# A hybrid layer and a conformer block on one core: another opening, with the norms as two numbers a row

## The reference, cut to what matters

```
h = rms_norm(x, pre_g)                       # x / sqrt(mean(x^2) + 1e-6) * g
a_u, a_v, a_g, b_x, b_g, x_q, x_g, gates = split(h @ w_in)
y_a = u * spatial_gating(layer_norm(a_v)) * silu(a_g)
y_b = s5(b_x) ... * silu(b_g)                # diagonal state space model, GLU
k, v = rms_norm(mem, mem_g) @ w_k, ... @ w_v # 4 heads of 256
y_x = softmax(x_q k^T / 16) v * silu(x_g)
x = x + rms_norm(sum(sigmoid(gates) * (y @ w_branch)) @ w_out, post_g)
then: x += conformer_conv(rms_norm(x)); x += sq_relu_mlp(rms_norm(x)); out = rms_norm(x)
```

## Time and profile before

| | |
|---|---|
| median of 3 runs | 2095.28 us (2091.62 to 2097.49) |
| the profiled execution | 2091.96 us, span 2090.2 us |
| PE busy | 2013.0 us, 96% |
| DVE, ACT, POOL busy | 1610.0, 976.4, 417.4 us |
| chain that ended last | PE 68%, DVE 23%, issue 4%, ACT 3% |
| mean DMA rate | 181 GB/s |

### The profile page before, as it was taken

The page is one execution under the profiler, slowest core; times in us unless marked ns, Lnnn a source line. Parts: engine busy times, 40 slices in busy tenths (PEclk is TensorE's granted clock), DMA queues, the critical chain, the costliest instruction groups (busy, mean ns, idle before and its releaser), DMA issues.

```text
span 2090.2 us, 30805 instructions
## 1 busy us (share of the span) xinstructions
PE 2013.0 (96%) x12118; PEld 1750.6 (84%) x12118; DVE 1610.0 (77%) x2538; ACT 976.4 (47%) x1439; POOL 417.4 (20%) x293
## 2 busy tenths in 40 slices
PE   7999999999989999999999999999999999999997
PEld 6787887788777788888799987888888888888886
DVE  7766888989899996687899984777567657756766
ACT  5544444444443445556544335544344434434442
POOL 3400233333333330000187754000000000000000
PEclk9999999999999999999999998999999999999998
DMA  7554554444444455566456654555555555555553
GB/s 290 203 181 161 191 182 161 141 162 154 162 149 160 153 182 181 189 213 201 154 168 192 204 184 145 185 188 191 191 191 189 188 190 190 192 191 188 189 190 119
DMA packets 106704, 378.01 MB, mean 181 GB/s; under 512 B 11968, under 2 KB 15808, under 8 KB 106560
## 3 DMA queue, kind: packets, MB, share of 16 engines
q1 hardware_dynamic: 106560, 376.04, 53.9%
HBM read 373.01 MB, written 2.98 MB: 180 GB/s over the span
## 4 chain that ended last, share of the span: by engine, by line
PE 68%; DVE 23%; issue 4%; ACT 3%; DMA 1%; SPq 0%; DVEq 0%; ACTq 0%
PE bank L1751 37%; PE bank L1753 19%; DVE wl L991 7%; DVE bank L1536 3%; ACT wh L635 2%; PE bank L1740 1%; PE bank L1742 1%; PE bank L1741 1%; PE bank L1756 1%; PE bank L1758 1%; PE bank L1757 1%; DVE scr L1022 1%; PE bank L1780 1%; DVE wm L1315 1%; DVE sq L998 1%
## 5 line engine op out<-in xcount | busy, mean ns | idle before, releaser
L991 DVE TENSOR_TENSOR wl<-raw,wh 128x1024 fp32r<-128x1024 f32 x593 | 742.2, 1256 | 335.2 <-ACT wh L635 334.1
L635 ACT ACTIVATE wh<-raw 128x1024 fp32r<-128x1024 f32 x680 | 710.7, 1054 | 517.4 <-PE bank L1753 369.7
L1751 PE MATMUL bank<-Hr,wh 128*128 128x512 f32 x2432 | 864.8, 399 | 15.8 <-DVE wl L991 12.1
L1751 PE MATMUL bank<-Yr,wh 128*128 128x512 f32 x2176 | 768.5, 397 | 20.9 <-DVE wl L991 12.2
L1753 PE MATMUL bank<-Hr,wl 128*128 128x256 f32 x2432 | 683.9, 281 | 0.0
L1753 PE MATMUL bank<-Yr,wl 128*128 128x256 f32 x2176 | 610.6, 281 | 0.0
L1751 PEld LDWEIGHTS bank<-Hr,wh 128*128 128x128 f32 x2432 | 458.4, 188 | 133.5 <-issue 12.7
L1751 PEld LDWEIGHTS bank<-Yr,wh 128*128 128x128 f32 x2176 | 409.7, 188 | 119.8 <-DVE wl L991 11.3
L1753 PEld LDWEIGHTS bank<-Hr,wl 128*128 128x128 f32 x2432 | 462.1, 190 | 0.3
L1753 PEld LDWEIGHTS bank<-Yr,wl 128*128 128x128 f32 x2176 | 412.6, 190 | 0.2
L578 POOL TENSOR_TENSOR wl<-raw,wh 128x1024 fp32r<-128x1024 f32 x87 | 215.4, 2485 | 417.5 <-ACT wh L635 388.5
(11 more groups left out here) (321 smaller groups left out, 1815.6 us busy)
## 6 DMA issues: line engine op xcount, KB each, us to landing
raw<-in_w_up SPq DMA_DIRECT2D x128, 512.0 KB, 3.2
raw<-in_w_dn SPq DMA_DIRECT2D x128, 512.0 KB, 3.3
raw<-in_w_g SPq DMA_DIRECT2D x96, 512.0 KB, 3.2
raw<-in_w_p SPq DMA_DIRECT2D x80, 512.0 KB, 3.3
raw<-in_w_b SPq DMA_DIRECT2D x48, 512.0 KB, 3.3
raw<-in_w_out SPq DMA_DIRECT2D x32, 512.0 KB, 3.3
raw<-in_w_bx SPq DMA_DIRECT2D x16, 512.0 KB, 5.2
raw<-in_w_q SPq DMA_DIRECT2D x16, 512.0 KB, 3.4
```

Of the source, the lines that this page charges most:

```text
L635: e.activation(wh[:, c % WN, :], raw[:, c % RAW, :], ACT.Copy).then_inc(s_hi, 1)
L991: e.tensor_tensor(wl[:, c % RAW, :], raw[:, c % RAW, :], wh[:, c % WN, :].bitcast(F32), ALU.subtract).then_inc(s_low_v, 1)
L1751: e.matmul(dst.rearrange("p (h t) -> p h t", h=2), lh, pair.both[:, :, k, :], start=first_part and kk == 0, stop=last_part and kk == 7, sk ...
```

## The change

The DMAs at the start go x 0-3, chunk 0, x 4-7, chunks 1, 2, x 8-11, chunk 3, x 12-15, chunks 4 to 6, constants. ACT does x 0-3, high(0), x 4-7, high(1), high(2), x 8-11, high(3), high(4), x 12-15, and all four squares at c = 1 and 2. The squares are folded only from 16 to 4 tiles, the two folds being hung on c = 3 and 4 (mem: 21 and 22); PE sums the rest with eight matmuls of one column (`mean_squares`, in front of chunk 6; mem: 23), which leaves one number per token on the partitions, two columns. Epsilon, root and reciprocal work on these 128 x 2 numbers; DVE puts them on a diagonal (`across`), PE spreads them over the partitions by one product with `ones` (in front of chunk 7; mem: 24) and ACT copies this as r_x or r_mem. q reads `hp0` like bx, and the norm is multiplied onto its results. bx tiles 0 to 2 get their norm at c = 8. The scaling of x runs at c = 8 to 13, 15, 17, 19, 21, that of mem at c = 30 to 39.

```
-RX = 5
-MEM_SQ, MEM_R = 17, 23
-MEM_N = 26
+RX = 7
+X_N = (8, 9, 10, 11, 12, 13, 15, 17, 19, 21)
+MEM_SQ, MEM_R = 17, 24
+MEM_N = 30
 # SP
         e.dma_start(Xf[:, 0:4, :], a["xT"][:, 0:4, :]).then_inc(s_x[0], 16)
+        chunk(0)
         e.dma_start(Xf[:, 4:8, :], a["xT"][:, 4:8, :]).then_inc(s_x[1], 16)
-        chunk(0)
         chunk(1)
+        chunk(2)
         e.dma_start(Xf[:, 8:12, :], a["xT"][:, 8:12, :]).then_inc(s_x[2], 16)
-        chunk(2)
+        chunk(3)
         e.dma_start(Xf[:, 12:16, :], a["xT"][:, 12:16, :]).then_inc(s_x[3], 16)
...
 # ACT
+        def norm_across(n, dst):
+            w.wait_ge(s_rb, n)
+            e.activation(dst, bank[7][:, 0:T], ACT.Copy, scale=2048.0).then_inc(s_rstd, 1)
...
             elif j.stage == "q":
-                w.wait_ge(s_hl, 8)
+                w.wait_ge(s_hl, 4)
...
+            for c in ((0,), (1, 2), (3, 4), ())[i]:
+                high(c)
...
+            if c in (1, 2):
+                for i in (2 * c - 2, 2 * c - 1):
+                    e.activation(sq0[:, 4 * i:4 * i + 4, :], Xf[:, 4 * i:4 * i + 4, :], ACT.Square).then_inc(s_xq, 1)
...
+            if c == RX:
+                w.wait_ge(s_cst, 16)
+                norm_across(1, r_x)
+            if c == RX - 1:
+                root(1, rs_x)
...
-                w.wait_ge(s_mm, end("bx", 7))
+                w.wait_ge(s_mm, end("q", 7))
                 e.activation(mp.hi[:, u:u + 2, :], Mf[:, u:u + 2, :], ACT.Copy).then_inc(s_mh, 1)
 # DVE
+        def squares_folded(n):
+            w.wait_ge(s_xq, 4 * n)
+            e.tensor_tensor(sq0[:, 0:8, :], sq0[:, 0:8, :], sq0[:, 8:16, :], ALU.add).then_inc(s_v, w.own())
+            yield
+            w.wait_ge(s_v, w.n)
+            e.tensor_tensor(sq0[:, 0:4, :], sq0[:, 0:4, :], sq0[:, 4:8, :], ALU.add).then_inc(s_sum, 1)
+
+        def norm_rows(n, v):
+            w.wait_ge(s_mean, n)
+            e.tensor_scalar(v, bank[7][:, 0:2], 1e-6, None, ALU.add).then_inc(s_eps, 1)
+            w.wait_ge(s_root, n)
+            e.reciprocal(v, v).then_inc(s_v, w.own())
+            w.wait_ge(s_v, w.n)
+            w.wait_ge(s_id, 1)
+            across(v, 0, s_xdg)
+
+        def times_norm(j):
+            w.wait_ge(s_comb, j.comb)
+            w.wait_ge(s_rstd, 1)
+            e.tensor_tensor(kept(j), kept(j), r_x, ALU.mult).then_inc(s_u, 1)
...
+            if c in (RX - 4, RX - 3):
+                next(x_folded, None)
             for j in ENDED.get(c, ()):
                 evac(j)
+            if c == RX - 1:
+                norm_rows(1, rs_x)
+            if c == RX:
+                w.wait_ge(s_cst, 16)
+            if c == RX + 1:
+                for t in range(8):
+                    if AT["bx", t].end <= RX:
+                        times_norm(AT["bx", t])
+            if c in X_N:
                 w.wait_ge(s_rstd, 1)
+                scaled(X_N.index(c), Xf, "pre", r_x, s_xn, s_hh, hp, s_hl)
+            if c in (MEM_SQ + 4, MEM_SQ + 5):
+                next(mem_folded, None)
+            if c == MEM_R - 1:
+                norm_rows(2, rs_mem)
 # PE
-        ACTS = {"bx": (hp0, s_x0l, 1, 0), "q": (hp, s_hl, 2, 0), ...
+        ACTS = {"bx": (hp0, s_x0l, 1, 0), "q": (hp0, s_x0l, 1, 0), ...
+        def mean_squares(n):
+            w.wait_ge(s_ones, 1)
+            w.wait_ge(s_sum, n)
+            w.wait_ge(s_rstd, n - 1)
+            for t in range(4):
+                ins = stats(sq0[:, t, :], 0, first_part=t == 0)
+            ins.then_inc(s_mean, 1)
+
+        def norm_across(n):
+            w.wait_ge(s_xdg, n)
+            e.matmul(bank[7][:, 0:T], ones, dg[:, 0:2, :], start=True, stop=True).then_inc(s_rb, 1)
...
+            if c in (RX - 1, MEM_R - 1):
+                mean_squares(1 if c == RX - 1 else 2)
+            if c in (RX, MEM_R):
+                norm_across(1 if c == RX else 2)
```

More of the change, by code:

```diff
@@ L402, in _build @@
     st = small[:, 32:64]
+    rs_x, rs_mem = st[:, 0:2], st[:, 2:4]
     mA = keep[0]
@@ L528, in sync @@
         e.dma_start(Xf[:, 0:4, :], a["xT"][:, 0:4, :]).then_inc(s_x[0], 16)
+        chunk(0)
         e.dma_start(Xf[:, 4:8, :], a["xT"][:, 4:8, :]).then_inc(s_x[1], 16)
-        chunk(0)
         chunk(1)
+        chunk(2)
         e.dma_start(Xf[:, 8:12, :], a["xT"][:, 8:12, :]).then_inc(s_x[2], 16)
-        chunk(2)
+        chunk(3)
         e.dma_start(Xf[:, 12:16, :], a["xT"][:, 12:16, :]).then_inc(s_x[3], 16)
+        for c in range(4, RAW):
+            chunk(c)
         e.dma_start(cst[:, 16:NCONST], a["cst"][:, 16:NCONST]).then_inc(s_cst, 16)
-        for c in range(3, RAW):
-            chunk(c)
         for c in range(1, NC + 1):
@@ L667, in evac @@
             elif j.stage == "k":
+                w.wait_ge(s_hl, 8)
                 half(j, KT[:, t, :])
@@ L905, in scalar @@
                 e.activation(hp0.hi[:, t, :], Xf[:, t, :], ACT.Copy, scale=cv("pre", t)).then_inc(s_x0h, 1)
[L906 to L912, removed]
+            for c in ((0,), (1, 2), (3, 4), ())[i]:
+                high(c)
         for c in range(1, NC + 1):
-            if c == RX:
-                root(1, r_x)
+            if c in (1, 2):
+                for i in (2 * c - 2, 2 * c - 1):
+                    e.activation(sq0[:, 4 * i:4 * i + 4, :], Xf[:, 4 * i:4 * i + 4, :], ACT.Square).then_inc(s_xq, 1)
             if c in (end("gt", 1), LAST_PAD):
@@ L918, in scalar @@
                     evac(j)
-            if c + 3 < NC and c + 3 not in HIGH_POST and c + 3 not in HIGH_LN:
+            if 4 < c + 3 < NC and c + 3 not in HIGH_POST and c + 3 not in HIGH_LN:
                 high(c + 3)
@@ L923, in scalar @@
                     evac(j)
-            if RX + 2 <= c < RX + 10:
-                u = 2 * (c - RX - 2)
+            if c == RX:
[3 more added lines that the diff above has]
+                root(1, rs_x)
+            if c - 1 in X_N[0:8]:
+                u = 2 * X_N.index(c - 1)
                 w.wait_ge(s_xn, u // 2 + 1)
@@ L930, in scalar @@
                 w.wait_ge(s_mem[i], 16)
-                w.wait_ge(s_rstd, 1)
-                e.activation(sq0[:, 4 * i:4 * i + 4, :], Mf[:, 4 * i:4 * i + 4, :], ACT.Square).then_inc(s_mq, 1)
+                w.wait_ge(s_mean, 1)
+                e.activation(sq0[:, 4 * i:4 * i + 4, :], Mf[:, 4 * i:4 * i + 4, :], ACT.Square).then_inc(s_xq, 1)
+            if c == MEM_R - 1:
+                root(2, rs_mem)
             if c == MEM_R:
-                root(2, r_mem)
+                norm_across(2, r_mem)
             if MEM_N + 1 <= c < MEM_N + 9:
@@ L1039, in evac @@
                 add_half(j, uT[:, t, :])
-                w.wait_ge(s_comb, j.comb)
-                w.wait_ge(s_rstd, 1)
-                e.tensor_tensor(uT[:, t, :], uT[:, t, :], r_x, ALU.mult).then_inc(s_u, 1)
+                if j.end > RX:
+                    times_norm(j)
             elif j.stage == "q":
@@ L1602, in vector @@
                                        ALU.mult, ALU.subtract).then_inc(s_x0l, 1)
[L1603 to L1608, removed]
+            for c in ((0,), (1, 2), (3,), ())[i]:
+                low(c)
+        x_folded, mem_folded = squares_folded(1), squares_folded(2)
         main_setup, main_scales = s5_setup(), s5_scales()
@@ L1612, in vector @@
                 low(c + 3)
-            if c == RX:
-                rstd(1, r_x, 1e-6)
+            if c in (RX - 4, RX - 3):
+                next(x_folded, None)
             for j in ENDED.get(c, ()):
                 evac(j)
-            if RX < c <= RX + 10:
-                w.wait_ge(s_rstd, 1)
[L1619 to L1624, removed]
+            if c == RX - 1:
[7 more added lines that the diff above has]
+            if c in X_N:
+                w.wait_ge(s_rstd, 1)
+                scaled(X_N.index(c), Xf, "pre", r_x, s_xn, s_hh, hp, s_hl)
+            if c in (MEM_SQ + 4, MEM_SQ + 5):
+                next(mem_folded, None)
+            if c == MEM_R - 1:
+                norm_rows(2, rs_mem)
             if MEM_N <= c < MEM_N + 10:
@@ L1696, in tensor @@
         w = Waits(e)
-        ACTS = {"bx": (hp0, s_x0l, 1, 0), "q": (hp, s_hl, 2, 0), "av": (hp, s_hl, 2, 0), "k": (mp, s_ml, 2, 0),
+        ACTS = {"bx": (hp0, s_x0l, 1, 0), "q": (hp0, s_x0l, 1, 0), "av": (hp, s_hl, 2, 0), "k": (mp, s_ml, 2, 0),
                 "v": (mp, s_ml, 2, 0), "au": (hp, s_hl, 2, 0), "ag": (hp, s_hl, 2, 0), "g0": (hp, s_hl, 2, 0),
@@ L1914, in tensor @@
                 w.wait_ge(s_tril, 1)
-                w.wait_ge(s_eps, 2)
+                w.wait_ge(s_rstd, 2)
                 if h == 1:
```

10 lines of the change are left out of this document (2 added, 8 removed).

## The result

The changed kernel takes 2108.57 us (median of 4, 2105.52 to 2109.39), the kernel before 2093.75 (4 runs, three of which gave the 2095.28 above): ratio 1.0066, 95% interval 1.0047 to 1.0086. The direction was forecast, the size not: 14.8 us in place of 5, outside the range (2088 to 2106). Slower by more than 0.3% had been given a chance of 0.25. The profiled execution took 2107.76 us with a span of 2106.0, 15.8 more than that of before.

What follows compares the result with a forecast made beforehand. PE, busy 96% of 2090.2 us, was taken to bound the kernel; -1.7 + 4.0 - 6.8 - 0.5 = -5.0 took the profiled execution from 2092.0 to 2097.0, 2100.3 at the median, range 2088 to 2106.

Steps and rivals of the forecast that it cites:

- the walk to mem's folds: Instruction order at mem, chunks 20 to 23: POOL low parts before and between the folds, second fold ending T22 + 7.8.
- the sign of being right: In the trace, PE waits 4 to 6 us for the folded squares at chunks 6 and 23.
- Start: Opening DMAs reordered: first matmul at 9.5 us in place of 10.47, 0.95 earlier; chunk 4's 1.4 us wait goes.
- First sum: Squares of x, chunk 6: PE idles 4.8 us, chunk 7 starts at 39.6 in place of 37.9, losing 1.7 us.
- q: q from raw activations: the wait for normed activations and the slow clock after it go, gaining 4.0 us (3.5 to 4.3).
- Second sum: Squares of mem, chunk 23: PE idles 5.0 us; loss 6.8 us, bounds 4.0 and 7.5.
- Bias rows: Mem tiles moved over c=38, where DVE makes the first bias rows: a low part goes ahead, loss 0.5 us.
- (a): At both sums DVE keeps the port between ready instructions: 1.7 us faster, 2093.6; 32% together with mixed orders and (d).
- (b): The folds hide altogether behind chunks: 6.8 us faster, 2088.5; chance 12%.
- (c): DVE enters c=8 with too little lead, PE waits for low parts before q: 9 us slower, 2104.3; chance 11%.
- (d): Only q gains, the two sums move nothing: 2095.6 us; 32% together with (a) and mixed orders.
- the branch where DVE keeps going: At the squares of x, second fold ends at 28.7, chunk 7 starts at 34.5 to 36: gains 2 to 3.5 us.

Runs made afterwards that it cites:

- busy-wait run: Changed kernel with 18 and 28 matmuls of unread result ahead of PE's waits for the folded squares at chunks 6 and 23: 2106.03 us, ratio 1.0055.
- q-only run: Kernel before with q from raw activations alone, norm multiplied onto its results, mem tiles at c=30 to 39: 2096.5 us, ratio 1.0002.
- no POOL: Changed kernel with the low parts of chunks 4 to 30 all made by VectorE, none by GpSimd: 2097.76 us, ratio 1.0014.
- folds first: Changed kernel with both folds back to back ahead of the low part of their step: 2104.77 us, ratio 1.0047.
- sums later: Changed kernel with the sum of x wanted two chunks later (RX=9) and that of mem three later (MEM_R=27): 2094.85 us, ratio 0.9995.
- no POOL with sums later: Changed kernel with RX=9 and MEM_R=27, and GpSimd's low parts of chunks 4 to 30 on VectorE, one-column statistics kept: 2086.52 us, ratio 0.9957.
- bias rows later: Changed kernel with later sums, no GpSimd low parts in the opening and wide mean, plus bias rows five chunks later (BIAS=41): 2084.57 us, ratio 0.9949.
- before without POOL: Kernel before with GpSimd making, of the low parts of chunks 4 to 30, only that of chunk 8: 2089.98 us, ratio 0.9974.
- the wide ones: Changed kernel with the four folded tiles summed by four matmuls of 256 columns and the norm 256 wide again: 2103.51 us, ratio 1.0044.

## Why the prediction was wrong, step by step

The mechanism was forecast: POOL's low parts between the folds, PE's waits for sq and the clock at 0.50 behind both. Two steps of the sum failed, and together they make 7.5 of the 10.8 us by which the traces miss it.

The first is a term that stands in the sum twice: the statistics at 1.8 us, a price read at full clock, and the slow clock of 1.5 and 1.2 us taken as if it followed them. The slow clock covers the statistics too: they took 3.4 us at both places, and chunks 6 and 23 took 5.0 and 4.8 in place of 2.8. At x that is 3.4 + 2.2 = 5.6 us against the forecast's 3.3, at mem 3.4 + 2.0 = 5.4 against 3.0: 4.7 us in all. The busy-wait run shows it for x: with PE kept busy the same eight matmuls take 1.8 us and the chunk 2.9.

The second is the walk to mem's folds, which had PE idle for 5.0 us; it idled 7.8, where the sign of being right was 4 to 6. The rest is chunks that landed 1.2 us late, 1.6 us far behind the opening, and small change. Term by term:

- **Start.** First matmul at 9.65 (forecast 9.5). Chunk 4's high part at 16.9 (15.7): the chunks landed 1.2 us later than pieces of 1.27 us from the earlier trace rows gave. POOL's part of it still hid.
- **First sum.** Folds in the forecast order with POOL between; PE idled 5.3 (4.8). Chunk 7 started at 43.2 (39.6; before 37.9): 5.3 lost, not 1.7. Some 2.3 of the 3.6 difference are the clock, and about 1.2 the late landing.
- **q.** From -5.3 at chunk 7 to -1.4 at T23 (88.8 against 87.4): 3.9 gained (4.0). Right as a number. But the gain leans on the loss: alone on the kernel before, the wait for Hr became waits for low parts, and 0.4 to 1.9 us was left (the q-only run). That DVE had its lead in the changed kernel because PE had stood still fits this, but no run shows it by itself.
- **Second sum.** PE idled 7.8 (5.0). The walk had DVE begin the first fold at T22 - 2.0; it began at T22 + 3.0 (89.1). ACT, held up by its waits for normed tiles and by four squares, made high(22) and high(24) 1.5 us late and more, so POOL's low(24) came ahead of the first fold, on the product of q1, and low(26) behind it. ACT's wait of 1.4 us for a normed tile at 79.2 is in part POOL's again: the DVE product at 76.1 took 2.28 for 0.4 of work. The second fold ended 2.7 later than forecast, at T22 + 10.5. With no POOL the wait is 2.8, so 5.0 of the 7.8 go with POOL's low parts, directly or by way of ACT. With 3.4 for the statistics and 2.0 more for chunk 23, ACT's first high part after the chunk goes from 92.23 to 105.07, that after T23 only from 87.53 to 88.91: 11.5 us lost in between, to which the second product adds 0.35 (forecast for both: 6.8).
- **Bias rows.** 1.4 against 0.8: 0.6 lost (0.5).
- **Later, 1.6 us**, is not in the opening: at a wait of 2.1 us for the attention's pT, the clock fell in the changed kernel and not in the one before. All twelve traces have this wait, of 1.8 to 2.1 us. In six of them (changed, folds first, sums later, no POOL with sums later, bias rows later, before without POOL) the clock fell, in the other six not. Both groups hold kernels with and without POOL's low parts. How often it falls for one kernel isn't known, as each was traced once; a median can carry up to 1.6 us of it. The stretches of the changed kernel (524 to 530) and of the one before (511 to 517):

```profile
524.00:530.00 6.00, 3.90 (x15) 2.94 (x14) 4.54 (x8) 3.23 (x6) 1.48 (x1) 0.79 0.38 135
```

```profile
511.00:517.00 6.00, 3.90 (x21) 3.20 (x20) 4.54 (x8) 3.24 (x6) 0.67 (x1) 1.00 0.27 91
```

Sum: 5.3 - 3.9 + 11.5 + 0.35 + 0.6 + 1.6 = 15.5 of 15.8.

Of the rivals, (a) needed DVE to keep the port: it didn't once at these sums where POOL had work ready, so the Trainium skill's rule ("SBUF — State Buffer", "SBUF: two separate sides": the one that starts first gets the pair) taken as first to ask described both sums; the row at 246.86 of before stays unexplained. The prediction's sum had a slip in the branch where DVE keeps going: its own terms put chunk 7 at 33.7 to 35.2 us, not at 34.5 to 36. It played no part, as the branch didn't come. (b) is what the kernel becomes with the sums wanted later and no POOL: 2086.5, where I had 2088.5 for it. (c) was nearest by its number (2104.3), but its mechanism didn't come: PE waited for no low part between chunks 8 and 20, and q gave its 3.9. (d) fell with the first wait for sq.

## What to carry to other kernels

Here a GpSimd low part cost VectorE 2.2 us, whenever VectorE had an instruction of this kind ready, to save it 1.15. Count such an instruction as VectorE work, and take it away where VectorE is short: that alone gave 5 us on the kernel before and 11 on the changed one. A reduction that another engine waits for needs its due time set by the worst order of what may fall between its steps, since a miss of 4.7 us or more cost, each time here, the wait and then everything up to the clock's return. And a gain measured behind a new stall has to be measured without the stall before it is believed.

## What the runs showed of the hardware that was not expected

- The length of a wait doesn't say whether the clock falls. In the opening it fell behind every wait of 2.4 us or more that one-column matmuls followed, and behind every one of 4.7 or more, but also behind 1.07 us and 1.8 us of one-column matmuls (no POOL, 0.63 in the stretch after) and behind 1.31 and 0.44 us (before, 0.50). It stayed at 1.00 behind 1.24 and 0.44 us at the same place of the same code (q from raw), behind 2.57 us (before without POOL) and behind 2.3 us (sums later). Without a wait, the same one-column matmuls left it at 1.00.
- Full clock came back 8.0 us after the one-column sums for x began, 4.8 after the wide ones began, both behind waits of about 5 us.
- Where GpSimd and VectorE both had work ready, they took turns at nearly every instruction of these sums, also between two VectorE instructions that don't depend on each other (4.50 and 3.36 us for 2.2 and 1.15 of work).
